# Delta stage of a two-block transformer kernel: the spreading of the running sums of the log decay, from one fp32 product per direction to two fp32r products over both

## The reference

```python
def gated_delta_rule_chunked(q, k, v, g, beta):
    g = jnp.cumsum(g.reshape(n, h, nc, c), axis=-1)              # running sums of the log decay in a chunk
    decay = jnp.exp(jnp.where(incl, g[..., :, None] - g[..., None, :], -jnp.inf))
    kb = k * beta[..., None]
    a_low = jnp.where(strict, jnp.einsum('nhcid,nhcjd->nhcij', kb, k) * decay, 0.0)
    tmat = lax.linalg.triangular_solve(eye + a_low, eye, left_side=True, lower=True, unit_diagonal=True)
    u = jnp.einsum('nhcij,nhcjv->nhciv', tmat, v * beta[..., None])
    w = jnp.einsum('nhcij,nhcjk->nhcik', tmat, kb * jnp.exp(g)[..., None])
    qk = jnp.einsum('nhcid,nhcjd->nhcij', q, k) * decay
    ...
```

## Time and profile before

| what | value |
|---|---|
| median of 3 runs | 4250.06 us (4238.54 to 4257.17) |
| profiled execution, its own time | 4250.56 us |
| its span | 4248.8 us |
| granted TensorE clock, mean of the span | 0.941 of 2.4 GHz |
| delta stage in that span | about 1036 to 1870 us |
| mean DMA rate over the span | 40 GB/s |

### The profile page before, as it was taken

The page is one execution under the profiler, slowest core; times in us unless marked ns, Lnnn a source line. Parts: engine busy times, 40 slices in busy tenths (PEclk is TensorE's granted clock), DMA queues, the critical chain, the costliest instruction groups (busy, mean ns, idle before and its releaser), DMA issues. The chain is left out here.

```text
span 4248.8 us, 48761 instructions
## 1 busy us (share of the span) xinstructions
PE 3807.2 (90%) x19208; PEld 3128.9 (74%) x19208; DVE 1625.1 (38%) x2316; ACT 1076.4 (25%) x1824; POOL 1275.3 (30%) x875
## 2 busy tenths in 40 slices
PE   4899999998999999998879999998797988888967
PEld 2777777767898989896757888886576767667746
DVE  8333333342444444441232323333252056663241
ACT  2334333332333333331121111111212022231132
POOL 0312112133221212123333343332323344444431
PEclk7999999999999999998999999999978989999988
DMA  3100001002000000001201111110321111111201
GB/s 126 38 25 26 30 25 30 25 20 88 6 16 6 12 10 11 8 31 54 87 20 50 44 49 44 49 44 26 119 52 32 47 39 40 35 37 45 90 19 64
DMA packets 50711, 172.44 MB, mean 41 GB/s; under 512 B 6136, under 2 KB 13688, under 8 KB 48768
## 3 DMA queue, kind: packets, MB, share of 16 engines
q1 hardware_dynamic: 50560, 170.34, 12.2%
HBM read 150.89 MB, written 19.42 MB: 40 GB/s over the span
## 5 line engine op out<-in xcount | busy, mean ns | idle before, releaser
L298 PE MATMUL DP<-XH,WH 128*128 128x512 f32 x2896 | 997.6, 426 | 179.8 <-POOL XL L387 67.6
L298 PE MATMUL DP<-XL,WH 128*128 128x512 f32 x2896 | 909.9, 396 | 0.0
L298 PE MATMUL DP<-XH,WL 128*128 128x512 f32 x2896 | 908.7, 395 | 0.0
L298 PEld LDWEIGHTS DP<-XH,WH 128*128 128x128 f32 x2896 | 533.2, 193 | 364.3 <-issue 228.8
L244 POOL CAST WH<-WRAW 128x1024 fp32r<-128x1024 f32 (+2 forms) x249 | 249.4, 1001 | 1733.5 <-issue 837.7
L298 PEld LDWEIGHTS DP<-XL,WH 128*128 128x128 f32 x2896 | 553.9, 191 | 120.7
L298 PEld LDWEIGHTS DP<-XH,WL 128*128 128x128 f32 x2896 | 552.9, 191 | 120.1
L246 POOL TENSOR_TENSOR WL<-WRAW,WH 128x1024 fp32r<-128x1024 f32 (+2 forms) x249 | 561.9, 2256 | 20.0
L779 DVE SCALAR_TENSOR_TENSOR SS<-B,RQ,SBI 128x256 f32<-128x256 f32 (+2 forms) x192 | 74.5, 430 | 376.5 <-PE B L484 376.5
L1233 PEld LDWEIGHTS DP<-PM,XX 128*128 128x128 f32 x1536 | 183.4, 195 | 19.2 <-issue 16.7
L1233 PE MATMUL DP<-PM,XX 128*128 128x64 f32 x1536 | 190.3, 278 | 5.5 <-ACT XX L1464 5.5
(11 more groups left out here) (416 smaller groups left out, 5301.3 us busy)
## 6 DMA issues: line engine op xcount, KB each, us to landing
WRAW<-in_w_up SPq DMA_DIRECT2D x44, 512.0 KB, 3.5
WRAW<-in_w_attn SPq DMA_DIRECT2D x36, 512.0 KB, 3.5
WRAW<-in_w_down SPq DMA_DIRECT2D x22, 512.0 KB, 3.4
XR<-in_x SPq DMA_DIRECT2D x2, 4096.0 KB, 13.7
WRAW<-in_w_dn SPq DMA_DIRECT2D x16, 512.0 KB, 3.2
WRAW<-in_w_lrux SPq DMA_DIRECT2D x10, 512.0 KB, 3.4
WRAW<-in_w_lrug SPq DMA_DIRECT2D x10, 512.0 KB, 3.5
WRAW<-in_w_bl SPq DMA_DIRECT2D x10, 512.0 KB, 3.3
```

What stands on the lines that cost most here:

```text
L298: mm = pe.matmul(DP[b.slot][:, half * H:half * H + H], w[b.slot][:, k, :], x[:, k, half * H:half * H + H], start=one, stop=end)
```

## The change

The running sums are spread by fp32r products. POOL makes a high part (GH, the log decays rounded to fp32r) and a low part (GL, the rest) once, before the first group, and a copy of ONES in fp32r (ONR). For each group it writes two masked tiles (RBS, high and low, both directions in each) with four instructions instead of two. PE adds the two products, of 512 columns each and over both directions, in the same PSUM bank. RB is no more written by POOL, only by DVE and ACT. POOL's wait before a spread changes from `dec_ready` (DVE has used RB) to `r_ready` (PE has used RBS).

```diff
         RB = [at(f"RB{e}", S0 + 8 + 2 * e, [P, 2, 2, P]) for e in range(2)]
+        RBS = [[at(f"RBS{e}{i}", 72 + 4 * e + 2 * i, [P, 2, 2, P], F32R) for i in range(2)] for e in range(2)]
+        GH, GL = at("GH", S0 + 47, [P, NT, 16], F32R), at("GL", S0 + 47.5, [P, NT, 16], F32R)
+        ONR = at("ONR", 153.25, [P, P], F32R)
...
@@ spread_g, PE
-                for d in range(2):
-                    mm = pe.matmul(PT_E[e][:, 256 * d:256 * d + 256], ONES, RB[e][:, d].rearrange("p h n -> p (h n)"),
-                                   start=True, stop=True)
+                for i in range(2):
+                    mm = pe.matmul(PT_E[e], ONR[:, :], RBS[e][i][:, :, :, :].rearrange("p d h n -> p (d h n)"),
+                                   start=(i == 0), stop=(i == 1))
                 mm.then_inc(r_ready, 1)
@@ spread, POOL
                 if n >= 2:
-                    pool.wait_ge(dec_ready, 2 * n - 2)
-                for d in range(2):
-                    i = 8 * d + 2 * p
-                    g = ABN[:, chunk(s, d), i:i + 2].rearrange("p (h k) -> p h k", k=1).broadcast_to([P, 2, P])
-                    x = pool.tensor_tensor(RB[e][:, d], twice(con("tri", d, P)), g, ALU.mult)
+                    pool.wait_ge(r_ready, n - 1)
+                for part_of, gs in zip(RBS[e], (GH, GL)):
+                    for d in range(2):
+                        i = 8 * d + 2 * p
+                        g = gs[:, chunk(s, d), i:i + 2].bitcast(F32).rearrange("p (h k) -> p h k", k=1).broadcast_to([P, 2, P])
+                        x = pool.tensor_tensor(part_of[:, d], twice(con("tri", d, P)), g, ALU.mult)
                 x.then_inc(rb_ready, 1)
@@ before spread(0), POOL
             pool.wait_ge(abn_ready, 1)
+            pool.tensor_copy(ONR[:, :], ONES)
+            pool.tensor_copy(GH[:, :, :], ABN[:, :, 0:16]).then_inc(g_parts, 1)
+            pool.wait_ge(g_parts, 1)
+            pool.tensor_tensor(GL[:, :, :], ABN[:, :, 0:16], GH[:, :, :].bitcast(F32), ALU.subtract).then_inc(g_parts, 1)
+            pool.wait_ge(g_parts, 2)
             spread(0)
             spread(1)
```

More of the change, by code:

```diff
@@ L966, in program @@
             "cv_mid", "cv_dve", "cv_silu", "dsq_ready", "ss_ready", "rt_ready", "rk_ready", "z_ready"))
-        k_turned, kn_ready, v_turned, vb_ready, st_zero = (once(n) for n in (
-            "k_turned", "kn_ready", "v_turned", "vb_ready", "st_zero"))
+        g_parts, k_turned, kn_ready, v_turned, vb_ready, st_zero = (once(n) for n in (
+            "g_parts", "k_turned", "kn_ready", "v_turned", "vb_ready", "st_zero"))
         rb_ready, r_ready, ex_ready, e_ready, g_ready, dec_ready, a_turned, aa_ready, x0_part, x0_ready, x_turned, \
```

## The result

The changed kernel took 4330.91 us in the median of 5 runs (4299.03 to 4333.46), the kernel before 4256.29 us (4238.54 to 4257.17, 5 runs): a ratio of 1.0164, 95% interval 1.014 to 1.0189, so slower by 1.6%. The forecast was 4272 us and the range ended at 4289. The profiled execution took 4299.03 us, the lowest of the five, with a span of 4297.2 us, 48.4 more than before.

What follows compares the result with a forecast made beforehand. Delta stage bound by PE's queue, POOL setting its pace at 15 waits: products -14.3, XX waits +17.1, start +2.3, clock +1.7 and +14.8, sum +21.6 us, so 4272 us (+0.51%), range 4252 to 4289.

Steps and rivals of the forecast that it cites:

- What bounds the stage: Delta stage, 1036 to 1870 us: bound by PE's queue, with POOL setting PE's pace at 15 waits for XX.
- The wait for XX: PE at L1196: longer spread ahead of the pair's second first level adds 1.14 us to 15 waits, 17.1 us more.
- The price of a mask: POOL's masks in spread: four take 2.32 us instead of two in 1.18, so 1.14 us more per group.
- the dear bound of 0.74: POOL's masks at 0.74 us each, as L246: four might take 2.95 us, 1.8 more per group.
- The start: Before spread(0): copies, subtraction and waits cost 1.2 us, plus 1.14 in spread(0); PE's first wait grows by 2.3 us.
- The saving on PE: spread_g, 32 groups: two fp32r products of 0.23 us replace the fp32 product, 14.3 us less.
- The clock: TensorE's clock falls after all 15 longer XX waits, 14.8 us more, and after the first wait, 1.7 us more.
- 29 us, if each fall is of the longer kind: Upper end for the clock term: 15 falls of 3.4 us less the present 22.2 us.
- deep falls: Rival, chance 0.20 together with dear masks: all 15 clock falls of the longer kind, +35.8 us, 4286 us.
- the clock does not care: Rival, chance 0.22: clock falls stay as they are, saving and delay cancel to +5.1 us, 4256 us.
- covered at L1196: Rival, chance 0.07: POOL's second first_level waits for ACT's AA anyway, hiding the longer spread; -10.3 us, 4240 us.
- The last rival: Chance 0.03: fp32r products run in fp32 passes, twice the present work, 32 x 0.9 us more, some 4315 us.

Runs made afterwards that it cites:

- e3: The kernel before with only POOL's order changed, both first levels of a pair ahead of the two spreads: ratio 0.9924 to before, 4221.57 us.
- e5: The changed kernel without the low part: POOL masks only the high part with two instructions, both PE products read it: ratio 0.9961 to before.
- e1: The changed kernel with PE's two spreading products made twice over in every group: ratio 1.0126 to before, 4313.75 us.
- e4: The kernel before, fp32 products kept, with POOL writing each masked tile twice, once into a tile nobody reads: ratio 1.0118 to before, 4302.97 us.
- e2: The changed kernel with POOL making both first levels of a pair ahead of the two spreads: ratio 0.9924 to before, 4224.74 us.
- e6: e2 with the two spreading products made twice over in steps 2 and 3 (first pairs): ratios 0.9907 and 0.9898 to before in two runs.
- e9: e6 with POOL's copies and first two spreads moved ahead of the second weight split: ratio 0.9888 to before, 4208.16 us.
- e10: The kernel before with e3's order and the first two spreads ahead of the second weight split: ratio 0.9898 to before, 4225.16 us.
- e7: The changed kernel with the two spreading products made twice over in steps 2 and 3 (first pairs) alone, long waits kept: ratio 1.0132 to before.
- e8: The changed kernel as it is, profiled a second time: 4318.77 us in one execution, stage 969.3 us.

## Why the prediction was wrong

- **What bounds the stage** was right: PE's queue, and POOL at 15 places.
- **The wait for XX**: 15 x 1.14 = 17.1 us forecast, 34.0 - 16.7 = 17.3 measured. That the masks stood ahead of the second first level, and that POOL never had to wait there, was right, and e3 shows the worth of the place itself.
- **The price of a mask**: 0.61 us as taken; the dear bound of 0.74 didn't come.
- **The start**: 2.3 us forecast, 2.6 measured, and a fall of 6.8 us behind it instead of 3.4.
- **The saving on PE**: 14.3 us forecast. e5, which has it with the start's 1.2 us and nothing else of weight, gives 12.6 at full clock for 13.1 worked out. The Trainium skill (TensorE: Matmul & The Clock Gate, "Back-to-back issue gap") has about 131 ns per product, and by the estimate from it the saving would have been 6 us larger. The runs side with the 230 ns of the trace or a little above: four products instead of two cost e1 16 us over 32 groups, 0.25 us each, and in the pair loop of the changed kernel two products hold PE for 0.54 us at full clock (below), so a group there saves 0.38 us and not 0.46, about 2 us of the 14.3:

```profile
1198.56 0.70 PE L1162 MATMUL B<-RBS,ONR 128*128 128x512 f32 x2
1199.10 1.89 PE L1212 MATMUL DP<-YY,AA 128*128 128x64 f32 x16
```

- **The clock: the step that failed.** I priced the falls at "15 x 2.5 = 37", 14.8 us more, and closed the bound with "29 us, if each fall is of the longer kind". The count was right in the first profile, 15 of 15. The length was not. I carried over the mean of nine falls behind waits of 1.2 us, and took the longest stretch in those rows, 6.8 us, for the longest possible. Measured: 147 us of low clock behind 15 falls in the first profile and 191 behind 11 in the second, 4.9 and 8.7 us lost per fall. With the other falls, the clock cost the stage 58.6 and 79.3 us where the forecast had 16.5. That is most of the miss: the profiled spans are 48.4 and 68.2 us over the one before, and the medians differ by 74.6.
- **Why the falls got longer** has two parts, and the range saw neither. The change halves the spreading products that stood behind the waits, and in first pairs the clock then stayed low for 20.5 to 23.9 us instead of 10.2 at most (8 falls against 18). And longer waits make falls more frequent and long ones possible behind the last waits, with the old stream too (e4: 163 us of low time, stretches of 27.3). Half the low time over before is 21 us for the stream alone (e5), 37 and 55 for the wait with a long stream (e1, e4), 59 and 79 for both. With two profiles of one kernel 21 us apart, these are sizes and not a sum; that the wait is the larger part is what they show.
- The rival "deep falls" named the right mechanism and was too small for the same reason; "the clock does not care" and "covered at L1196" are refuted by the waits and by e4. The last rival, fp32r products run as fp32 ones, has the number nearest to the result, 4315 us, by luck: there are 64 records and not more, and PE's products got shorter.
- What stays open is why, of two waits alike, one gives 3.4 and another 27.3 us, behind the last waits above all. The two profiles of one kernel differ in it, and no run here controlled it.

## What to carry to other kernels

In a stage of small matmuls, where TensorE's clock falls behind short waits as here, two edits have a price that no instruction shows: work put ahead of something PE waits for, and a long product made shorter behind such a wait. Before shortening a product, ask what it does for the clock of the small ones around it; and if an idle engine sets the pace at fixed places, move what nobody needs soon behind what PE waits for: here that alone was worth 0.8%, and it turned a change that lost 1.6% into part of the fastest version.

## What the runs showed of the hardware

- PE, never idle, stayed at 1.2 GHz for 23.9 us in a first pair of the change. After two short groups of 512 columns, the last at 1110.61, it ran only products of 64 and 128 columns for 14 us, and the clock was back 2.3 us behind the start of the products of 256 columns; the three other first pairs show the same. That a fully busy engine stays at half clock I had not expected. Behind last waits the clock came back without such products, after up to 27.3 us.
- Behind a wait of 1.0 to 1.2 us in this stage the clock fell in about half of the cases (9 of 15 before, 9 of 15 in e5, 9 of 24 at the waits for YY of e2, e3, e6, e9 and e10). Behind 2.1 to 2.3 us it was 15 of 15 (change, e1, e4), 13 of 15 (e7) and 11 of 15 (e8).
- POOL's product with an fp32r output takes as long as with an fp32 one here: 614 ns against 612 for 128x256.
- Two profiled executions of the changed kernel, 4299 and 4319 us, differ by 20.6 us in this stage, half of their difference in low time.
